# The attention products of a step stand together in front of one block of projection products, and projections run around the first logits

## What is computed

```python
h = rms_norm(x, norm_mix_g[l])
proj = h @ w_in[l]                       # q, k, v (8 heads x 2 maps x 64; v 8 x 128) and pool channels
logits = einsum('bqhmd,bkhmd->bmhqk', qb, kb) * scale      # per block of 128 queries, keys up to its end
logits = where(allowed, logits + bias, -inf)               # T5 bias, chunks of 64
p = softmax(logits); w = p[:, 0] - lam * p[:, 1]
a = einsum('bhqk,bkhd->bqhd', w, v)
a = rms_norm(a, subln_g[l]) * (1.0 - lam_init); y_a = a.reshape(B, S, -1) @ w_attn_up[l]
g = sigmoid(h @ w_gate[l] + b_gate[l])                     # first half gates y_a, second the pool branch
```

## Time and profile before

| | |
|---|---|
| median of 3 runs | 1885.22 us (1882.05 to 1885.58) |
| profiled execution, its own time | 1880.56 us |
| its span | 1878.8 us |
| busy: PE, DVE, ACT, POOL | 94%, 74%, 58%, 29% |
| chain that ended last: PE's share | 88% |
| attention stage, first pool product to first product of the up-projection | 116.2 to 307.2 us |

### The profile page before, as it was taken

The page is one execution under the profiler, slowest core; times in us unless marked ns, Lnnn a source line. Parts: engine busy times, 40 slices in busy tenths (PEclk is TensorE's granted clock), DMA queues, the critical chain, the costliest instruction groups (busy, mean ns, idle before and its releaser), DMA issues.

```text
span 1878.8 us, 23411 instructions
## 1 busy us (share of the span) xinstructions
PE 1763.3 (94%) x8235; PEld 1417.2 (75%) x8235; DVE 1395.8 (74%) x1246; ACT 1086.5 (58%) x1004; POOL 552.5 (29%) x438
## 2 busy tenths in 40 slices
PE   5989999999897969899999999999999999999992
PEld 4867767888784747688888888888888888888872
DVE  4434463345423758799999999999999999999994
ACT  4134554235224226677677677677677677777762
POOL 4001221000000007344334334335335335335321
PEclk9999999999999979999999999999999999999996
DMA  9221114235330428899999999999999999999983
GB/s 312 83 90 57 56 57 174 90 112 186 128 93 1 174 91 333 315 347 378 383 373 380 381 372 380 378 373 381 380 375 376 383 372 379 381 373 378 381 310 107
DMA packets 111062, 501.36 MB, mean 267 GB/s; under 512 B 9365, under 2 KB 9434, under 8 KB 78154
## 3 DMA queue, kind: packets, MB, share of 16 engines
q1 hardware_dynamic: 98752, 459.30, 63.4%
q0 software_dynamic: 10784, 36.46, 7.6%
q10 hardware_dynamic: 1482, 5.01, 0.7%
HBM read 478.40 MB, written 22.34 MB: 267 GB/s over the span
## 4 chain that ended last, share of the span: by engine, by line
PE 88%; DVE 3%; POOL 3%; issue 2%; ACT 2%; DMA 1%; ACTq 0%; DVEq 0%; SPq 0%; POOLq 0%
PE ps L1823 35%; PE ps L1843 18%; PE ps L1483 7%; PE ps L1485 7%; PE ps L1484 7%; PE ps L1609 2%; POOL slot_table L679 2%; PE ps L1607 2%; PE ps L1611 2%; PE ps L1812 2%; PE ps L1634 1%; PE ps L1792 1%; PE ps L1801 1%; PE ps L1742 1%; PE ps L1674 1%
## 5 line engine op out<-in xcount | busy, mean ns | idle before, releaser
L1305 DVE TENSOR_TENSOR wlo<-raw,whi 128x2048 fp32r<-128x2048 f32 x380 | 851.3, 2285 | 75.1 <-ACT whi L961 75.1
L961 ACT ACTIVATE whi<-raw 128x2048 fp32r<-128x2048 f32 x380 | 717.8, 1913 | 152.9 <-PE ps L1823 152.9
L641 POOL TENSOR_TENSOR mark<-ident 1x1 f32<-1x1 f32 x32 | 289.0, 9030 | 321.0 <-ACT ybuf L983 321.0
L1823 PE MATMUL ps<-whi,xhi 128*128 128x512 f32 x1024 | 286.7, 402 | 0.3 <-DVE xlo L1310 0.3
L1823 PE MATMUL ps<-wlo,xhi 128*128 128x512 f32 x1024 | 274.8, 390 | 0.0
L1823 PE MATMUL ps<-whi,xlo 128*128 128x512 f32 x1024 | 274.4, 390 | 0.0
L1823 PEld LDWEIGHTS ps<-wlo,xhi 128*128 128x128 f32 x1024 | 193.2, 189 | 41.3
L1823 PEld LDWEIGHTS ps<-whi,xhi 128*128 128x128 f32 x1024 | 191.6, 190 | 41.9 <-DVE xlo L1310 1.2
L1823 PEld LDWEIGHTS ps<-whi,xlo 128*128 128x128 f32 x1024 | 192.2, 188 | 40.6
L1053 DVE TENSOR_TENSOR wlo<-raw,whi 128x2048 fp32r<-128x2048 f32 x52 | 117.6, 2289 | 139.8 <-ACT whi L725 139.4
L1843 PE MATMUL ps<-whi,ahi 128*128 128x512 f32 x512 | 164.6, 403 | 0.0
(11 more groups left out here) (319 smaller groups left out, 2485.0 us busy)
## 6 DMA issues: line engine op xcount, KB each, us to landing
raw<-in_w_gu SPq DMA_DIRECT2D x256, 1024.0 KB, 8.5
raw<-in_w_down SPq DMA_DIRECT2D x128, 1024.0 KB, 7.4
raw<-in_w_in SPq DMA_DIRECT2D x14, 1024.0 KB, 7.3
raw<-in_w_gate SPq DMA_DIRECT2D x8, 1024.0 KB, 5.1
raw<-in_w_xkv SPq DMA_DIRECT2D x8, 1024.0 KB, 5.1
raw<-in_w_attn_up SPq DMA_DIRECT2D x4, 1024.0 KB, 4.9
raw<-in_w_out SPq DMA_DIRECT2D x4, 1024.0 KB, 5.4
raw<-in_w_xq SPq DMA_DIRECT2D x4, 1024.0 KB, 7.0
```

The lines of the kernel that those rows point to most:

```text
L641: g.tensor_tensor(mark[:, 0:1], ident[0:1, 0:1], ident[0:1, 1:2], ALU.add)
L961: s.activation(whi[:, m % RING, :], raws[m % RAWS], ACT.Copy).then_inc(hi_done, 1)
L1305: v_.tensor_tensor(wlo[:, m % RING, :], raws[m % RAWS], whi[:, m % RING, :].bitcast(F32), ALU.subtract).then_inc(lo_done, 1)
L1823: mm = t_.matmul(ps[:, n, :], a[:, k, :], w[:, slot, n * 512:(n + 1) * 512], start=False, stop=k == KT - 1 and a is xlo)
```

## The change

TensorE's pass becomes logits(it+1), transposes(it-1), value products(it-2), and then all of the pass's projection products in one block. The table becomes 16 a pass and starts two passes early, so that `filled(-1)` is 16: 8 projection products stand ahead of the wait for the pool read and 8 behind logits(0). ScalarE's pass puts the copy (now of step it-2) and the square ahead of the exp, reads tiles by `filled(it - 2)` and turns a head one pass later. VectorE makes W ahead of the scale. Units 10 and 11 are split inside the loop, at most one unit a pass, on both engines when `filled(it - 2)` allows it.

```diff
-    return min(17 * max(min(it + 1, 17), 0) + 9 * max(it - 16, 0), CHUNK_MMS * len(FILL))
+    return min(16 * max(min(it + 2, 18), 0) + 9 * max(it - 16, 0), CHUNK_MMS * len(FILL))
...
 ScalarE
-                v[:, 0:4, i, :], b.rearrange("p (h d) -> p h d", h=4), ACT.Copy))
+                v[:, 0:4, i, :], b.rearrange("p (h d) -> p h d", h=4), ACT.Copy), held_back=2)
...
             for it in range(STEPS + 4):
-                (exp of step it)
-                st = it - 1
+                st = it - 2
                 (copy of wtsT for st, then the square of step it - 3)
-                if it % TT == 0 and it >= 2 * TT:
+                (exp of step it)
+                if it % TT == 1 and it > 2 * TT:
                     turn_head(it // TT - 2)
-                while read < 4 * len(FILL) and filled(it - 1) >= TILE_MMS * (read + 1):
+                while read < 4 * len(FILL) and filled(it - 2) >= TILE_MMS * (read + 1):
                     read_tile(read)
                     read += 1
-                while prepared[0] < FILL[-1].end_unit + RING and filled(it - 2) >= unit_filled(prepared[0] - RING):
+                if prepared[0] < FILL[-1].end_unit + RING and filled(it - 2) >= unit_filled(prepared[0] - RING):
                     prep(prepared[0])
                     prepared[0] += 1
...
 VectorE
-            prep_to(OF["v"][0].end_unit + RING)
...
                 (z of step it)
+                (W of step it - 1)
                 (scale of step it - 4)
-                (W of step it - 1)
-                while prepared[0] < FILL[-1].end_unit + RING and filled(it - 3) >= unit_filled(prepared[0] - RING):
+                if prepared[0] < FILL[-1].end_unit + RING and filled(it - 2) >= unit_filled(prepared[0] - RING):
                     prep_to(prepared[0] + 1)
...
 TensorE
-            pe.wait_ge(dve_emptied, OF["pm"][0].emptied)
...
+            fill_to(filled(-1) // 2)
+            pe.wait_ge(dve_emptied, OF["pm"][0].emptied)
             logits(0)
+            fill_to(filled(-1))
...
             for it in range(STEPS + 2):
-                third = (filled(it) - filled(it - 1)) // 3
                 if it + 1 < STEPS:
                     logits(it + 1)
-                fill_to(filled(it - 1) + third)
                 (transposes of it - 1)
-                fill_to(filled(it - 1) + 2 * third)
                 (value products of it - 2)
-                if it < STEPS:
-                    fill_to(filled(it))
+                fill_to(filled(it))
```

More of the change, by code:

```diff
@@ L835, in _ @@
                                  ).then_inc(asq_ready, 1)
-                if it % TT == 0 and it >= 2 * TT:
+                if it < STEPS:
+                    n = P * (QTS[it % TT] + 1)
+                    act.wait_ge(z_ready, 2 * it + 2)
+                    for m in range(2):
+                        s.activation(zexp[:, it % 2, m, 0:n], zexp[:, it % 2, m, 0:n], ACT.Exp, scale=-1.0,
+                                     bias=att[:, it % 8, m:m + 1], accum_out=att[:, it % 8, 4 + m:5 + m]
+                                     ).then_inc(exp_ready, 1)
+                if it % TT == 1 and it > 2 * TT:
                     turn_head(it // TT - 2)
-                while read < 4 * len(FILL) and filled(it - 1) >= TILE_MMS * (read + 1):
+                while read < 4 * len(FILL) and filled(it - 2) >= TILE_MMS * (read + 1):
                     read_tile(read)
                     read += 1
-                while prepared[0] < FILL[-1].end_unit + RING and filled(it - 2) >= unit_filled(prepared[0] - RING):
+                if prepared[0] < FILL[-1].end_unit + RING and filled(it - 2) >= unit_filled(prepared[0] - RING):
                     prep(prepared[0])
                     prepared[0] += 1
+            while read < 4 * len(FILL):
+                read_tile(read)
+                read += 1
             turn_head(HEADS - 1)
@@ L1166, in _ @@
                                                 ).then_inc(z_ready, 1)
[L1167 to L1172, removed]
                 st = it - 1
@@ L1185, in _ @@
                                             in1=zexp[:, b, 0, 0:n], op0=ALU.mult, op1=ALU.add).then_inc(w_ready, 1)
+                st = it - 4
+                if 0 <= st < STEPS:
+                    h, qt = st // TT, QTS[st % TT]
+                    dve.wait_ge(ascale_ready, st + 1)
+                    v_.tensor_scalar(qa[:, h, qt * P:(qt + 1) * P], ps[:, 3 + st % 2, 0:P], ascale[:, st:st + 1], None,
+                                     ALU.mult).then_inc(av_read, 1)
                 if it % TT == 1 and it > 2 * TT:
                     turn_head(it // TT - 2)
-                while prepared[0] < FILL[-1].end_unit + RING and filled(it - 3) >= unit_filled(prepared[0] - RING):
+                if prepared[0] < FILL[-1].end_unit + RING and filled(it - 2) >= unit_filled(prepared[0] - RING):
                     prep_to(prepared[0] + 1)
```

## The result

The changed kernel takes 1874.87 us, median of 6 runs (1870.82 to 1878.04), beside 1883.62 us (1881.51 to 1885.58, 6 runs) for the kernel before: ratio 0.995, 95% interval 0.9936 to 0.9965. It is faster by 8.8 us where 5.7 us were forecast. The profiled execution took 1871.53 us with a span of 1869.8 us, against 1880.56 and 1878.8 us before.

What follows compares the result with a forecast made beforehand. Mostly TensorE's own products bound the kernel. Gone 7.75 + 2.3 + 4.16 + 1.0 = 15.2 us, new 2.1 + 7.4 = 9.5 us, net 5.7 us faster: 1879.5 us median, range 1874 to 1884.5.

Steps and rivals of the forecast that it cites:

- Outside the attention stage the change touches nothing: Code outside the stage of 119.69 to 306.36 us stays untouched; time won or lost in the stage reaches the end almost whole.
- The lead-in, 7.75 us gone, 2.1 back: Stage start, around logits(0) and logits(1): 5.3 us idle and 2.45 us of half clock go; late splits give back 2.1 us.
- the wait at z(2): TensorE waits 1.7 us for VectorE's exp input of step 2, behind the split of unit 11.
- The 0.2 us at z(1): TensorE loses 0.2 us waiting for VectorE's exp input of step 1, behind the split of unit 10.
- The waits of 1.2 and 0.3 us go: TensorE's loop waits for projection tiles unread by ScalarE vanish, as ScalarE looks up the projection count of two steps ago.
- W no longer stands behind GpSimd's scale: VectorE scales behind the weights W, so TensorE's three short W waits, 0.8 us, go.
- Switches 0, pitch 1.0 us: TensorE's steps: grouping saves nothing at changes of product kind; closer spacing of projection products saves 1.0 us.
- Waits that come, 3.1 + 4.3 us: New TensorE waits where hi and lo splits share a step: 3.1 us at steps 18/19, 4.3 us at 28/29.
- A: Rival: TensorE's clock falls behind a new wait, 2.45 us each; one fall gives 1882.0 us, two 1884.4; chance 0.17.
- B: Rival: the switch behind logits goes and part of the split chain hides, 10.4 us gained, 1874.8 us; chance 0.17.
- C: Rival: VectorE's in-order wait for hi decides at all ten splits, 6.3 us slower than before, 1891.5 us; chance 0.09.
- D: Rival: the wait before logits(1) stays unfilled, unit 8 or the bank not ready; gain 2.1 us, 1883.1 us; chance 0.03.

Runs made afterwards that it cites:

- g1_no_leadin: The changed kernel with the old table, units 10 and 11 split ahead of the loop, no projection products before pass 0; 1883.15 us, ratio 1.0007.
- e4_leadin: The kernel before with only the table of 16, 8 + 8 products around logits(0), and units 10 and 11 split in the loop; 1875.29 us, ratio 0.9963.
- f3_lag_read: The changed kernel with VectorE's split one pass later and ScalarE's tile reads looked up one pass ago again; 1869.70 us, ratio 0.9924.
- f2_lag_scale: The changed kernel with VectorE's split one pass later and VectorE's scale ahead of W again; 1867.09 us, ratio 0.9907.
- f1_lag_thirds: The changed kernel with VectorE's split one pass later and TensorE's projection products in three groups a pass again; 1870.99 us, ratio 0.9922.
- e2_after_sel: The changed kernel with GpSimd's two selection copies moved ahead of its wait for the slot table; 1869.50 us, ratio 0.9941.

## Why the prediction was right, and where it was not

**Direction and size.** The median lies in the range, 4.6 us below the forecast; 1.6 us of that is the kernel before, whose six runs have a lower median than the three that the forecast started from. In the stage 5.7 us were forecast and 6.28 measured; most of the rest of the miss is outside it. That the stage came so near is partly luck: 3.0 us of slow clock that the sum left out were made up by 1.7 us less idle time and by pitch and switches that gave 2.5 to 2.8 us and not 1.0. The sentence "Outside the attention stage the change touches nothing" was true of the code and not of the time: the earlier trace rows stop at 460 us, and the 6.99 us wait at 765 us in the profile of before was not read. Whether it comes depends on where VectorE stands when the slot table's transfers are through, and that can shift with any edit.

**The lead-in, 7.75 us gone, 2.1 back.** Right. TensorE is busy from 119.77 us on; the wait at z(2) is 1.61 us (1.7 forecast) and the W behind it 0.26 (0.2). The 0.2 us at z(1) did not come. Of the net 5.65 us, the two kernels with and without it show 7.6 and 6.1. The excess of the first is mostly 1.8 us of tile waits and the 1.7 us of slow clock behind 235.0 us, which g1_no_leadin has and the change has not, less 1.4 us that the slow clock behind z(30) costs the change more. In e4_leadin 7.75 us are gone, 3.15 + 1.7 come back at z(2), and 1.5 us of tile waits and 1.2 us of later logits' waits go as well: 5.6 of the 6.1 us.

**"The waits of 1.2 and 0.3 us go" by ScalarE's lookup of two steps ago.** The waits went, the reason failed. With the old lookup they are gone in f3_lag_read and in e4_leadin; they stay in g1_no_leadin, which has the new lookup. What the two kernels without these waits have, and g1_no_leadin has not, is the lead-in: the table of 16 a pass from two passes earlier and the two splits inside the loop. Which of these removes them was not separated. They also come back (1.7 us) when the thirds are restored on ScalarE's new order; what in that order does it was not separated.

**"W no longer stands behind GpSimd's scale", 0.8 us.** The W waits fell from 2.1 us in four to 0.7 in two, but with the old order of W and scale the stage is as long in the lagged form (f2_lag_scale). VectorE's wait for the scale fell from 51.7 us to 5.0. What it did in the change itself was not tried. But the three short W waits (0.8 us) stay in e4_leadin, which has the old orders and thirds, and are gone both in f2_lag_scale (old order of W and scale) and in f1_lag_thirds (thirds): neither the order nor the grouping is needed for that by itself. ScalarE's new order, which all kernels without these waits share, was not undone alone.

**Switches 0, pitch 1.0 us.** Too low. The late steps show it (changed kernel, TensorE, the logits of two successive passes and the products behind them):

```profile
252.56 0.70 PE L1634 MATMUL ps<-kT,qa 64*128 64x256 f32 x4
253.19 0.33 PE L1662 MATMUL ps<-ident,wts 128*128 128x128 f32 x1
253.36 0.83 PE L1675 MATMUL ps<-v,wtsT 128*128 128x128 f32 x6
253.95 0.48 PE L1607 MATMUL ps<-hThi,whi 128*128 128x512 f32 x1
...
256.18 0.92 PE L1634 MATMUL ps<-kT,qa 64*128 64x384 f32 x4
```

The pass takes 3.62 us. The pass of the same widths before starts with the last line of the earlier trace rows and ends with this one, 3.69 us later:

```profile
265.04 0.92 PE L1634 MATMUL ps<-kT,qa 64*128 64x384 f32 x4
```

Over 31 passes 0.07 to 0.08 us are some 2.3 us, an estimate, where I had 1.0; the thirds restored cost 2.4 us beside their waits. By the starts in the two passes, the nine projection products take 2.23 us and not 2.45: the earlier trace rows show 0.34 and 0.32 us behind a short group where a run has 0.23, and three groups have three such places, one block has one. The transposes and value products, now in a row, take 0.76 us and not 0.61, so most of it is given back. I had named both effects and set them to 0. The 1.0 us also rests on a slip: 4.13 - 1.27 - 0.77 is 2.09 us and not 2.07, or 0.232 us a product, and the upper bound then is 2.5 us and not 1.5.

**Waits that come, 3.1 + 4.3 us.** Right in place and nearly in size: 1.22 + 0.41 + 0.99 = 2.62 us at 18/19, and 3.32 us of 3.65 at z(30). The chain was as long as drawn, 7.5 us from the end of z(29) at 268.19 to the logits at 275.67 us (7.3 forecast). TensorE's own work beside it was longer, 4.1 us and not 3.65: the smaller waits of the pair (0.65 us forecast) are not listed, but the transposes start 0.78 us behind logits(30) where the same widths take 0.63. Idle time was to be 9.5 us and is 7.8.

**The rivals.** A happened: the clock fell behind the 3.32 us wait, for 3.0 us, not 2.45. It was hidden in the total by terms that I had too small. Its chance of 0.17 was too low: in the stage every wait above 3 us in these kernels (3.15, 3.32, 3.34, 4.24 us) was followed by half clock. The Trainium skill, "TensorE: Matmul & The Clock Gate", "Why this matters for your kernels", which warns of idle gaps between bursts, had it right against my argument that the wait was shorter. But the length of one wait is not all that decides it. In the changed kernel 1.22 and 0.41 us at 227 us left the clock at 1.00 (226 to 236 us); the same two waits in g1_no_leadin were followed by half clock, and so was one of 1.69 us at 769.00 us of the changed kernel (granted 0.50 from 770 to 772 us), while 1.71 us at the same place in e2_after_sel was not. What tells them apart stays open. B was right only in the 0.07 us a pass; the chain of the splits hid nothing more. C fell: VectorE does wait for hi at all ten splits (21.6 us), but TensorE waits for it at none of steps 7, 8, 13 and 14. D fell.

**Sum of the stage.** Lead-in 7.75 gone and 1.87 back (z(2) and W(2)); tile waits 1.5 and W waits 0.8 gone; split waits 4.16 gone and 5.94 back; slow clock 3.0 back; pitch 2.5. That makes 5.9 us of 6.28; with the 2.8 us that the subtraction leaves for pitch it would be 6.2.

## What to carry to other kernels

Where an in-order engine waits for another one's result, ask it for that result a step later than the other makes it: here one pass of lag was worth more (8.9 us of stage) than the whole rearrangement (6.3 us). Split a change into its parts before crediting it: nearly all of the net gain was 16 products placed where TensorE stood idle, the grouping's 2.5 to 2.9 us were spent again by the splits in the same pass, and two of the edits, undone on top of the lag, did nothing measurable. Read the longest waits of the whole trace, also where the code stays the same; a collision that depends on timing can move by as much as the change.

## What the runs showed of the hardware

A GpSimd copy of 0.28 us took 9.72 us beside four VectorE subtractions with two operands in SBUF (8.88 us in a row) and ended with the last of them; the five kernels in whose profile it was the selection's copy waited 7.0 to 7.3 us on TensorE. The Trainium skill, "SBUF — State Buffer", "Terms", says that VectorE and GpSimd share a port pair that is held for a full instruction while the other blocks. The blocking agrees, though no run here shows the port itself; that it lasted over four instructions is more than that sentence says.

The clock came down within a wait or a little over a microsecond after it: in the changed kernel it was at 0.50 when the products resumed at 275.67 us, in e4_leadin the logits at 135.09 us still ran at full clock and the fall came at about 136.2 us, and in g1_no_leadin it came at about 235.0 us, behind waits of 1.22 and 0.41 us that ended at 232.78 and 233.69 us. The price was 3.0, 1.7 and 1.7 us.
